# A transformer block on one core: expert routing begun in the mixing part, tables built by partition, operands loaded ahead

## What is computed

```python
a = rms_norm(h, g_mix)
gq, ..., sk, sv = split(a @ w_in)                    # projections
o = concat([gla_mixer(...), dsa_mixer(...), swa_mixer(...)])
h = h + o @ w_out                                    # mixing part
# routing: one of 4 groups, in it the best 2 of 8 experts
g_w, g_sel = top_k(softmax(x @ w_rg + b_rg), 1)
e_w, e_sel = top_k(softmax(e_logits of group g_sel), 2)
order = argsort(expert); row = pad_start[e] + rank - start[e]   # blocks of 128 rows
y = for each block: (silu(xb @ w_gate[e]) * (xb @ w_up[e])) @ w_down[e]
h = h + gate-weighted y
e = rms_norm(p @ w_ple, g_ple)                       # embeddings
h = h + e * sigmoid(h @ w_ple_gate);  out = rms_norm(h, g_final)
```

## Time and profile before

| | us |
|---|---|
| median of 3 runs (lowest, highest) | 2921.84 (2920.48, 2926.15) |
| the profiled execution, device time | 2930.01 |
| its span, first to last instruction | 2928.3 |

### The profile page before, as it was taken

One profiled execution on the slowest core, in us unless ns is written; L12 is line 12 of the kernel. 1 busy time (PEld: TensorE's weight loads), 2 busy tenths in 40 slices (PEclk: granted clock), 3 DMA queues, 4 the chain that ended last, 5 costly groups with the idle time before them and its releaser, 6 DMA issues. The chain is left out here.

```text
span 2928.3 us, 34607 instructions
## 1 busy us (share of the span) xinstructions
PE 2620.2 (89%) x10900; PEld 1651.9 (56%) x10901; DVE 1798.5 (61%) x2347; ACT 1272.5 (43%) x2289; POOL 922.9 (32%) x923
## 2 busy tenths in 40 slices
PE   6988769999967888788699969999999999998998
PEld 3634323345833444444488836666666666665787
DVE  2186999599966666676422277754654446643676
ACT  2376858959855566665422132222222222221322
POOL 2376868500011111111100014433533445342321
PEclk9999989999978989998699979999999999999999
DMA  5101130112152022222444277895595555974664
GB/s 147 61 30 49 28 58 29 51 53 70 63 168 76 27 67 69 66 91 65 148 160 146 107 271 262 331 357 206 199 367 206 206 206 204 357 278 153 200 217 135
DMA packets 221503, 438.05 MB, mean 150 GB/s; under 512 B 22920, under 2 KB 91080, under 8 KB 221256
## 3 DMA queue, kind: packets, MB, share of 16 engines
q1 hardware_dynamic: 199432, 357.78, 35.6%
q0 software_dynamic: 13312, 47.32, 5.2%
q10 hardware_dynamic: 8640, 31.46, 2.6%
HBM read 331.14 MB, written 105.38 MB: 149 GB/s over the span
## 5 line engine op out<-in xcount | busy, mean ns | idle before, releaser
L2388 DVE CAST p_high<-p_low 128x2048 fp32r<-128x2048 f32 x128 | 204.1, 1594 | 392.1 <-PE p_psG L2479 292.7
L688 PE MATMUL p_psP<-home,p_ring 128*128 128x512 f32 x832 | 366.4, 598 | 0.0
L2495 PE MATMUL p_psY<-p_wd,p_hT 128*128 x752 | 332.6, 595 | 2.2 <-ACT p_hT L2551 1.9
L2390 DVE TENSOR_TENSOR p_low<-p_low,p_high 128x2048 fp32r<-128x2048 f32 x128 | 318.0, 2484 | 4.4
L688 PEld LDWEIGHTS p_psP<-home,p_ring 128*128 128x128 f32 x832 | 157.3, 192 | 205.1 <-issue 205.0
L2495 PEld LDWEIGHTS p_psY<-p_wd,p_hT 128*128 128x128 f32 x752 | 139.9, 191 | 161.6 <-issue 161.5
L717 PE MATMUL p_psI<-p_kI,p_qI 64*128 64x512 f32 (+3 forms) x608 | 149.2, 600 | 65.8 <-ACT p_relu L579 65.8
L2416 POOL TENSOR_TENSOR p_xT_low<-p_xT,p_xT_high 128x512 fp32r<-128x512 f32 x94 | 185.0, 1987 | 3.6 <-ACT p_xT L2536 3.6
L2477 PE MATMUL p_psG<-p_high,p_xT_high 128*128 128x512 f32 x376 | 166.7, 443 | 16.0 <-DVE p_low L2390 8.5
L786 DVE TENSOR_SCALAR_CACHE_REDUCE p_equal<-p_S_low,p_flip 128x512 uint8<-128x512 f32 (+4 forms) x139 | 168.6, 1213 | 0.0
L593 ACT ACTIVATE p_relu<-p_relu,p_small 128x512 f32<-128x512 f32 (+3 forms) x266 | 161.5, 662 | 0.0
(11 more groups left out here) (409 smaller groups left out, 5613.7 us busy)
## 6 DMA issues: line engine op xcount, KB each, us to landing
p_low<-in_w_expert_gate_dram SPq DMA_DIRECT2D x32, 2048.0 KB, 13.5
p_low<-in_w_expert_up_dram SPq DMA_DIRECT2D x32, 2048.0 KB, 17.1
p_wd<-in_w_expert_down_dram SPq DMA_DIRECT2D x32, 2048.0 KB, 10.8
y_dram<-p_y ACTq DMA_DIRECT2D x47, 512.0 KB, 8.2
p_xt<-in_x_dram SPq DMA_DIRECT2D x32, 512.0 KB, 4.8
y_dram<-p_clear SPq DMA_DIRECT2D x32, 512.0 KB, 4.7
proj_f<-p_stage SPq DMA_DIRECT2D x52, 256.0 KB, 2.4
p_ot<-o_dram SPq DMA_DIRECT2D x16, 512.0 KB, 4.6
```

What stands on the lines that cost most here:

```text
L688: mm = pe.matmul(psP[0:n, i % 2, :], w, aT[:, k, c * CH:(c + 1) * CH], start=k == 0, stop=k == KD - 1)
L2388: dve.tensor_copy(high[:, m, k, :], low[:, par, m, k, :].bitcast(F32)).then_inc(high_done, 1)
L2390: dve.tensor_tensor(low[:, par, m, k, :], low[:, par, m, k, :].bitcast(F32), high[:, m, k, :].bitcast(F32), ALU.subtract).then_inc(w_split, 1)
L2495: mm = pe.matmul(psY[:, c, :], hT[:, k, :], wd[:, bass.ds(at, 1), k, c * CH:(c + 1) * CH].rearrange("p a f -> p (a f)"), start=k == 0, sto ...
```

## The change

1. **Choice of experts.** The choice is made by a class `Picks` in batches of four tiles: three batches on DVE inside `mix`, after the norm of tiles 5, 9 and 13, the last one at the start of `route`. A batch is 19 instructions of 4 to 128 elements per partition.
2. **Ranks and positions.** The running sum over tiles is taken before the product; PE sums both in one accumulation (`rank`). The one-hot tables are built by 64 small instructions, one for each tile and choice, with no wait between them. Positions of both choices are read in one step.
3. **Tables.** Each partition counts for its own index, three instructions of 32 elements; three products with the identity turn the columns into one row of 384 numbers (`table`). The gates move to `experts`: two exponentials on ACT at its start, five small instructions on DVE behind its loop.
4. **Embeddings.** `EARLY` is 7: the seventh tile is made at the end of `project_and_select`, and `route` has six (3 to 8). Their operands go to a buffer `plate`, which first holds w_out, and are loaded at the end of `mix`. `route` begins with the weights of the experts, and the wait for copies between them is gone.
5. **Mixers' loads.** The scores of tiles 2 to 7 lie in a tile `near` of their own. Once their masks are stored, eight loads (`early`) go there from inside the projection's row of stores. `ahead` keeps eight; seven (`behind`) come after the first two masks in `mixers`.

```diff
-EARLY = 6
+EARLY = 7
...
-LOW = 12
+MIDDLE, LOW = 8, 12
...
+                if i == len(products) - 40:
+                    sp.wait_ge(first_masks, 16 * (MIDDLE - SCORED[0]))
+                    sp.wait_ge(rows_stored, 32)
+                    for m, c in ((m, c) for m in (5, 6) for c in (0, 1)):
+                        q = through[place["f", m, c]]
+                        sp.wait_ge(stored[q % NSTAGE], 16 * (q // NSTAGE + 1))
+                    operands.early(sp)
...
-                pool.dma_start(mask_dram[j, :, 0:width(j)], scores_of(S_low, S_high, j).bitcast(U8)[:, 0:width(j)]).then_inc(mask_stored, 16)
-            pool.wait_ge(mask_stored, 16 * NT)
+                pool.dma_start(mask_dram[j, :, 0:width(j)], scores_of(S_low, S_high, j).bitcast(U8)[:, 0:width(j)]).then_inc(first_masks if j < MIDDLE else mask_stored, 16)
+            pool.wait_ge(mask_stored, 16 * (2 + NT - MIDDLE))
...
-        self.load_qA(sp, 0)
         self.load_qS(sp, 0)
         sp.dma_start(tiles["kS"], self.proj_f[F_SK:F_SK + SKV * HD, :]).then_inc(self.loaded["kS"], 16)
+        self.load_g(sp, 0)
+        sp.dma_start(tiles["vS"], self.proj_t[:, T_SV:T_SV + SKV * HD].rearrange("(j p) d -> p j d", p=P)).then_inc(self.loaded["vS"], 16)
+    def behind(self, sp):
+        self.load_qS(sp, 1)
+        self.load_g(sp, 1)
+        self.load_gate(sp, 0)
+    def early(self, sp):
+        tiles = self.tiles
+        self.load_qA(sp, 0)
+        self.load_qA(sp, 1)
         for dst, src in ((tiles["wa"], self.w_alpha[0]), (tiles["ba"], self.b_alpha.rearrange("a p -> p a")), (tiles["gn"], row_broadcast(self.g_norm, GV))):
             sp.dma_start(dst, src, allow_slow_non_contiguous=True).then_inc(self.loaded["g_const"], 16)
-        self.load_g(sp, 0)
         sp.dma_start(tiles["nearA"], toeplitz(self.bias_rows, 0, AH)).then_inc(self.loaded["nearA"], 16)
         sp.dma_start(tiles["nearW"], toeplitz(self.bias_rows, AH, SH)).then_inc(self.loaded["nearW"], 16)
         sp.dma_start(tiles["sink"], row_broadcast(self.sinks, SH)).then_inc(self.loaded["nearW"], 16)
-        sp.dma_start(tiles["vS"], self.proj_t[:, T_SV:T_SV + SKV * HD].rearrange("(j p) d -> p j d", p=P)).then_inc(self.loaded["vS"], 16)
-        self.load_qA(sp, 1)
-        self.load_qS(sp, 1)
-        self.load_g(sp, 1)
-        self.load_gate(sp, 0)
...
+            loads.behind(sp)
             sp.wait_ge(clear_set, 1)
...
+        after(reduce(gm, G, AX, ALU.max))
+        after(tt(self.vg[:, t, :], G, across(gm, NG), ALU.subtract))
+        first_of(eg[:, :, :], G, gm, NG, eg[:, :, :], ALU.not_equal)
+        after(stt(out=em[:, :, :].rearrange("p j (g e) -> p j g e", e=EPG), in0=eg[:, :, :].unsqueeze(3).broadcast_to([P, B, NG, EPG]), scalar=NEG,
+                  in1=E.rearrange("p j (g e) -> p j g e", e=EPG), op0=ALU.mult, op1=ALU.add))
+        for i in range(2):
+            if i:
+                after(stt(out=em[:, :, :], in0=self.oh[:, 0, t, :], scalar=3.0 * NEG, in1=em[:, :, :], op0=ALU.mult, op1=ALU.add))
+            after(reduce(self.m[i][:, t], em[:, :, :], AX, ALU.max))
+            first_of(self.oh[:, i, t, :], em[:, :, :], self.m[i][:, t], NE, ve[:, :, :], ALU.is_equal)
+        after(tt(self.both[:, :, t].rearrange("p e j -> p j e"), self.oh[:, 0, t, :], self.oh[:, 1, t, :], ALU.add))
...
+                if t == NT - NB:
+                    sp.wait_ge(w_split, KD)
+                    load_ahead(sp)
...
+                if t in CHOOSE_AT:
+                    dve.wait_ge(r_copied, t)
+                    picks.choose(dve, after, scratch, picks.BATCH * CHOOSE_AT.index(t))
...
+CHOOSE_AT = (5, 9, 13)
+LAST = NT - EARLY
...
+            def rank():
+                pe.wait_ge(made, 7)
+                pe.wait_ge(step, BOTH_AT)
+                pe.matmul(psA[:, :], before[:, :], both[:, :, :].rearrange("p e j -> p (e j)"), start=True, stop=False)
+                pe.wait_ge(step, BOTH_AT + 1)
+                pe.matmul(psB[:, 0:NE], ones[:, :], run[:, :, NT - 1], start=True, stop=True).then_inc(counted, 1)
+                pe.matmul(psA[:, :], ones[:, :], run[:, :, :].rearrange("p e j -> p (e j)"), start=False, stop=True).then_inc(ranked, 1)
+            def place():
+                pe.wait_ge(step, COUNTS_READ_AT)
+                for c in range(2):
+                    pe.wait_ge(within, (2, 3)[c] * NT)
+                    if c == 1:
+                        pe.wait_ge(beyond, NT)
+                    for j in range(NT):
+                        mm = pe.matmul(psB[:, 0:NBX], in_block[:, c, j, :], of_block[:, c, j, :], start=(c, j) == (0, 0), stop=(c, j) == (1, NT - 1))
+                mm.then_inc(slotted, 1)
+            def table():
+                pe.wait_ge(step, TABLES_AT)
+                for i in range(3):
+                    mm = pe.matmul(psA[0:1, i * P:(i + 1) * P], cols[:, i:i + 1], ident[:, :], start=True, stop=True)
+                mm.then_inc(tabled, 1)
+            pe.wait_ge(p_loaded, 32)
             turn(OWN)
             for t in range(OWN, LAST):
                 if t + 1 < LAST:
                     turn(t + 1)
                 product(t)
-                if t == OWN + RANKED_AT:
-                    pe.wait_ge(made, 7)
-                    pe.wait_ge(step, BOTH_AT)
-                    a = both[:, :, :].rearrange("p j e -> p (j e)")
-                    pe.matmul(psA[:, :], before[:, :], a, start=True, stop=True).then_inc(ranked, 1)
-                    pe.matmul(psB[:, :], ones[:, :], a, start=True, stop=True).then_inc(ranked, 1)
-                if t - OWN in PLACED_BESIDE:
...
+            picks.choose(dve, after, scratch, NT - picks.BATCH)
+            assert n == BOTH_AT
...
+            after(dve.tensor_tensor_scan(flat(run), flat(reset), flat(both), 0.0, ALU.mult, ALU.add))
...
+            def in_blocks(c):
+                for j in range(NT):
+                    tsc(in_block[:, c, j, :], iota16[:, :], row_f[:, 0, c, j:j + 1], None, ALU.is_equal).then_inc(within, 1)
+            def of_blocks(c, done):
+                for j in range(NT):
+                    tsc(of_block[:, c, j, :], iota16[:, 0:NBX], row_f[:, 1, c, j:j + 1], token_f[:, j:j + 1], ALU.is_equal, ALU.mult).then_inc(done, 1)
+            in_blocks(0)
+            of_blocks(0, within)
+            of_blocks(1, beyond)
+            in_blocks(1)
...
+            dve.wait_ge(slotted, 1)
             after(dve.tensor_copy(slots[:, :], psB[:, 0:NBX]))
             assert n == SLOTS_AT
-            after(tt(cmpb[:, :, :], over(full[:, :], NBX, 1), over(iota[:, 0:NBX], NE, 2), ALU.is_le))
-            after(dve.tensor_reduce(be[:, 0:NBX], cmpb[:, :, :], AX, ALU.add))
-            after(tsc(last[:, :], order[:, NE - 1:NE], -1.0, None, ALU.add))
-            after(tsc(be[:, 0:NBX], be[:, 0:NBX], last[:, :], None, ALU.min))
-            after(tsc(be[:, NBX:NBX + 1], nbi[:, NE - 1:NE], -2.0, None, ALU.add))
-            after(dve.tensor_copy(blocks[:, 0:NBX + 1], be[:, :]))
-            after(dve.memset(blocks[:, NBX + 1:NBX + 3], 0))
-            after(tt(cmpb[:, 0:NE, :], over(order[:, :], NE, 1), over(iota[:, 0:NE], NE, 2), ALU.is_le))
-            after(dve.tensor_reduce(full[:, :], cmpb[:, 0:NE, :], AX, ALU.add))
-            after(tsc(full[:, :], full[:, :], float(NE - 1), None, ALU.min))
-            after(dve.tensor_copy(blocks[:, NBX + 3 + NE:NBX + 3 + 2 * NE], full[:, :]))
-            after(tt(cmpb[:, 0:NE, :], over(order[:, :], NE, 1), over(iota[:, 1:NE + 1], NE, 2), ALU.is_le))
-            after(tt(cmpb[:, 0:NE, :], cmpb[:, 0:NE, :], over(nb[:, :], NE, 1), ALU.mult))
-            after(dve.tensor_reduce(full[:, :], cmpb[:, 0:NE, :], AX, ALU.add))
-            after(dve.tensor_copy(blocks[:, NBX + 3:NBX + 3 + NE], full[:, :]))
...
+            after(tsc(junk[:, 0, :], start[:, :], token_f[:, 0:1], None, ALU.is_le, ALU.add, accum_out=cols[:, 0:1]))
+            after(tsc(junk[:, 1, :], order_of, token_f[:, 0:1], None, ALU.is_le, ALU.add, accum_out=cols[:, 1:2]))
+            after(stt(out=junk[:, 2, :], in0=order_of, scalar=below[:, :], in1=full[:, :], op0=ALU.is_le, op1=ALU.mult, accum_out=cols[:, 2:3]))
+            after(tsc(cols[:, 0:1], cols[:, 0:1], last[:, :], None, ALU.min))
+            after(tsc(cols[:, 1:2], cols[:, 1:2], float(NE - 1), None, ALU.min))
+            assert n == TABLES_AT
+            after(tsc(blocks[0:1, ROUNDS:ROUNDS + 1], nbi[0:1, NE - 1:NE], -2.0, None, ALU.add))
+            dve.wait_ge(tabled, 1)
+            after(dve.tensor_copy(blocks[0:1, 0:3 * P], psA[0:1, 0:3 * P]))
...
+RANKED_BEHIND, PLACED_BEHIND = 1, 4
...
+            dve.wait_ge(gate_raised, 2)
+            after(dve.tensor_reduce(gw[:, :], picks.vg[:, :, :], AX, ALU.add))
+            after(dve.tensor_scalar(total[:, :], ratio[:, :], 1.0, None, ALU.add))
+            after(dve.tensor_tensor(total[:, :], total[:, :], gw[:, :], ALU.mult))
+            after(dve.reciprocal(gates[:, 0, :], total[:, :]))
```

(5 more changed lines are left out.)

340 lines of the change are left out of this document (166 added, 174 removed).

## The result

| | median us | lowest to highest | runs |
|---|---|---|---|
| before | 2921.93 | 2920.48 to 2926.15 | 4 |
| changed | 2904.8 | 2903.34 to 2905.72 | 4 |

The ratio is 0.9939 (95% interval 0.9921 to 0.9956): 17 us less. The forecast was 2908.4 (-13.4 us), with a range of 2901 to 2916. Timed a second time, the changed one took 2905.37 us (0.9943, 0.993 to 0.9957).

What follows compares the result with a forecast made beforehand. DVE was taken to bound routing, with 7.3 us of cover before ACT, and ACT the projection's end. Terms of -11.4 in routing and -2 around the mixers' start sum to -13.4: median 2908.4 us, range 2901 to 2916.

Steps and rivals of the forecast that it cites:

- Choice of experts: Routing's start on DVE: last batch takes 5.4 us, ends 7.7 us earlier; three batches in the mixing part cost nothing.
- Ranks: Routing: PE's rank lets DVE go on 6.8 us earlier; the one-hot tables begin 11.7 us earlier.
- One-hot tables: Routing on DVE: 64 instructions without waits at 0.14 us each take 9 us, bounds 5 and 16.
- the pair: Two neighbouring DVE instructions of 2 elements in the trace, starting 0.08 us apart though each is listed at 0.17.
- Tables: Routing: list of tokens copied 12.3 us earlier, DVE ends 22.5 us earlier; the moved gates cost nothing.
- What is late next: Routing's end: last embedding product (5.9 us) and its store (3.5 us) end the stage, leaving -11.4 us.
- Seventh tile, mixers' loads: Projection's end and mixers' start: stage end +0.4 us, mask loads land in 2.3 instead of 5.5; sum -2.
- rival E: Projection: SP's early loads jam and stall ACT, then PE; slower than before, 2931 us at a 40 us hold; 3%.
- C: Embedding stores slow (6.4 us) in routing and at the projection's end: +2.9 and +3.3, 2914 us; 13%.
- D: Routing: PE's clock stays up for the last embedding product, store lands in 2.6 us: -3.2, 2905 us; 17%.
- B: One-hot tables: small instructions without waits cost as much as dependent ones, 16 us, 7 more: 2915.4 us; 14%.
- F: Mixing part: the choice isn't covered, up to 16 us come back: 2924 us; 3%.

Runs made afterwards that it cites:

- experiment 7: Changed kernel with the list's 32 one-hot instructions reduced to the comparison, without the product with the token: 2901.7 us, ratio 0.9913.
- experiment 5: Changed kernel with a wait behind each of the 64 one-hot instructions: 2909.39 us, ratio 0.9953.
- experiment 6: Changed kernel with its 64 one-hot instructions put back into six large ones: 2901.78 us, ratio 0.9934.
- experiment 4: Changed kernel with all first loads of the mixers issued in one piece at the projection's end, seventh embedding tile kept: 2910.42 us, ratio 0.9956.
- experiment 1: Kernel before, unchanged, profiled again: 2923.56 us, ratio 0.9993; its piece, one mixer result store to the next, took 28.5 or 25.6 us across profiles.
- experiment 2: Changed kernel with PE's last embedding product (tile 8) ahead of the list and table products: 2901.09 us, ratio 0.992.
- experiment 8: Changed kernel with all four batches of the choice at the routing stage's start, none in the mixing part: 2917.52 us, ratio 0.9982.

## Why the prediction was right, and where it was not

Its sum was -11.4 in routing, -2 around the mixers' start, and nothing elsewhere. Measured there are -10.3 and -3.2, -13.5 together against -13.4. That these two misses cancel is luck, and the 4 us by which the time was lower than forecast are none of its terms.

- **Choice of experts.** Right. The last batch ended 5.7 us after the stage's start, forecast 5.7 (1695.3 - 1689.6). The cover in the mixing part held: in the changed kernel a batch ran from 1527.35 to 1532.87, the residual half behind it came 2.1 us late, the next one at its usual time.
- **Ranks.** Right within 1 us: DVE went on 11.6 us after the start, forecast 12.3, and the one-hot tables began at 16.8, forecast 17.8.
- **One-hot tables.** Mis-sized: 11.9 us instead of 9. The step that failed is "I take **0.14**, nearer to the pair": they are 0.19 apart in the mean. I took half of the instructions as 33 elements long; they are 66. And I priced a second pointer operand with its operation at nothing, where it costs 0.06 us (experiment 7). That instructions without waits overlap was right (experiment 5: 0.29 and 0.34 us with a wait, 0.168 and 0.210 without), but six large ones take 9.5 us where the 64 take 11.9 (experiment 6). The Trainium skill, "VectorE: DVE Perf Modes", section "Rules for kernel authors", asks for few instructions, and these 9.5 against 11.9 us agree with it. By the same page's section "The DRAIN you can't avoid" a semaphore behind each instruction costs nothing extra; here the waits cost 8.2 us, so for these instructions the measurement decides against it. That section also says that an instruction which is not held starts earlier, and the 64 without waits do; the prediction left that sentence out.
- **Tables.** The list was there after 30.1 us, forecast 28.3: the 2.9 us from above, less the 1 us gained on the ranks. DVE was done after 33.6, forecast 30.9, since it waited 1.4 us for the table product, forecast 0.7.
- **What is late next.** Right, and this step carried the forecast: of the 20 us that DVE gained, the stage kept 10.3. The product took 5.16 us (5.9), the store 2.6 (3.5), which gave back most of what the tables lost: 43.6 us instead of 42.5. What I did not name is that a second thing stood 2.7 us ahead of it, the gather behind full DMA queues.
- **Seventh tile, mixers' loads.** The waits went as forecast: the store's issue came 3.65 later (24.90 to 28.55), from that issue to the end of the stage it is 3.2 us (6.9 to 7.0), from there to the first logits 2.34 (5.3 to 5.5). That sums to -3.2, forecast -2; its own parts, +0.4 and 2.3 for 5.5, make -2.8, so it was summed too low. Only for the first part is the cause shown: with the loads back in one piece the stage's end is late again (+4.3), the mask is not (+0.5, experiment 4). SP's early loads jammed nothing (rival E): 4.0 us for all eight.
- **What was missed.** 4 us by the medians. The table of the stages, by the means of two profiles a kernel, has 9 us beyond the 13.5: 3.5 in the mixers behind the first mask, 4 ahead of the embeddings, 1.9 in the experts, less 0.4 in the mixing part. Which of these the medians keep, two profiles can't say. Of the mixers' share about 1 us is there by their first third, where the loads' place still acts (experiment 4), and I had taken its effect to end with the first mask. For the rest there is only the piece of experiment 1, where PE's granted clock dips and 2.9 us go; the kernel of experiment 2 has that dip too and its mixers still took 582.5 us, so that dips make up the rest is not shown. The kernel before had its mixers at 589 us in both profiles, and whether the change is the cause of the fewer dips is open; so are the projection part and the experts.
- **The rivals.** C (slow landings) is refuted by the landings of 2.6 us in both places. D was the nearest by its time, 2905, and for half its reason: the store did land in 2.6. B was wrong in mechanism, since waits would have made the tables 20.1 us (experiment 5), but by size the 11.9 us lie between my 9 and its 16. F (the choice not covered) fell with experiment 8.

## What to carry to other kernels

When a stage ends with its last engine, list what every engine and queue still has to do at the new end, not only the one that was late: here the tables were done at 1710.3, a gather landed at 1716.8 and the embedding store at 1719.5, so 20 us on the bound were worth 10, and the further steps 0.6 to 4.1 each. Work whose result is not needed soon should not stand behind the critical products in an in-order queue, nor weights ahead of the small transfers that end a stage: the product in a hole of PE, two weight loads behind the stage and six large instructions for 64 small ones took 7.6 us more off the stage. And before a difference is explained, cut both profiles by stage and take a second profile of the same kernel.
